# Sparse attention rewritten to work on pairs of heads, with a pair's fifth chunk of transposes in the second PSUM bank, copied by VectorE

## The chip, the cores and the metric

One core of a Trainium2 chip runs the whole program. Its engines are TensorE (PE in the profile, its weight loads PEld), VectorE (DVE), ScalarE (ACT), GpSimd (POOL) and SyncE (SP, which issues the DMAs). The metric is the device time of one execution in microseconds, the median of several; lower is better.

## What is computed

A stack of layers on 512 tokens of width 1024, all in float32. The change lies in the second layer, whose attention has three branches for 16 heads of width 64 in two groups of keys and values, and beside them an attention of 4 heads on 256 memory rows:

```python
def nsa_layer(x, mem, ...):
    h = rms_norm(x, norm_g) @ w_in
    q, kv, gate_logits, z, qm, zm = split_cols(h, NSA_IN_SPLITS)
    ...
    k_cmp = compress_tokens(kc, pe_k, phik_w1, phik_w2)
    v_cmp = compress_tokens(vc, pe_v, phiv_w1, phiv_w2)
    o_cmp, p_cmp = compressed_attention(q, k_cmp, v_cmp, slopes)
    o_slc = selected_attention(q, ks, vs, p_cmp, slopes)
    o_win, _ = banded_attention(q, kw, vw, slopes, WIN_SIZE - 1, 1)
```

Every branch is softmax(q k^T / 8 - slope x distance) v with causal masking. With 512 tokens the selection takes all 8 blocks and the window covers all keys, so "selected" and "window" are both plain causal attention, with keys ks and values vs, and kw and vw. The compressed branch has 31 block keys. The branches are gated and summed, then multiplied by silu(z) and by the output weights.

## The kernel before

Stages follow one another, each closed by a barrier of all engines. Ahead of the attention stand a projection stage, which fills the query tiles q_stack, the keys ks and kw, the values vs and vw, the gates and yT (silu of z), and the stage compress, which makes k_cmp and v_cmp. Behind it stands output_product, the product with the output weights.

**Float32 by parts.** TensorE multiplies in a rounded float32 format in one pass. To keep accuracy a tensor is split into a high part and a low rest. Before, q_stack holds one tile for each head, its high part in partitions 0 to 63 and its low part in 64 to 127 (stack_halves), and a key tile holds its high part twice and its low part twice (twice_halves). A score tile then takes two matmuls over 128 partitions (stacked_scores).

**Units.** nsa_attention makes a list of units and hands it to column_attention with n_sets 1, lag 3, n_buf 4. A unit of kind "table" is one head in one branch: scores of four token tiles of 128, 256, 384 and 512 keys in PSUM banks 0 to 2, scanned by VectorE (add the distance table, take the maximum, one instruction for each tile, L1145), exponentials by ScalarE in place (L1233), reciprocal of the sums times the gate by VectorE (L1184, L1186), scaling by GpSimd (L1299), ten 128x128 transposes by TensorE (L1070) in three chunks in banks 3 to 5, two of which VectorE copies to SBUF (L1201) and one ScalarE (L1253). After two heads the value products of both follow (L1090), on half the columns of the array each. "cmp" is the compressed branch of four heads at once; "plain" is a memory head, scanned at L1150.

What sets the order on TensorE is the loop of passes. In pass k it does:

```python
pe.wait_ge(ready, cnt.pieces[k - n_sets + 1])   # in scores(k): all tiles of unit k - 1 scanned
...
scores(k); turn(k - lag); product(k - lag - 1)
```

VectorE does scan(k), weigh(k - 1), copy(k - lag), finish(k - lag - 1), and where head.at names the pass a split of output weights or of y rows (L228). finish multiplies a finished pair by silu(z) (L1384). GpSimd also builds each head's distance table (L2164). In the first four passes TensorE runs 16 idle_products, matmuls on the identity whose result nobody reads (L168). SyncE issues the zero fill of the expert rows, after unit 20 the first output weights into the free query tiles (load_head), and after the last product the second ones (start_second).

**The head of the next product.** At the end the stage does the first k row of the output product, 12 matmuls (begin_head, L160 to L162). output_product then does rows 1 and 2, runs its rider (transposes of mem_rows, which its own DMA loads first, L2220), and goes on with weights that VectorE rounds and splits (L173, L175).

A later stage, diff_attention, is written in the other style: units of two 64-row score sets, the matmuls of the two in alternation on different halves of the rows (L2341), scans at L2420, in the order DIFF_PAIRS.

## Time and profile before

| | us |
|---|---|
| median of 3 runs | 2972.87 |
| the runs | 2964.62 to 2975.65 |
| the profiled execution | 2974.96 |
| its span, first to last instruction | 2973.0 |
| mean granted TensorE clock | 0.986 of full |

Over the span TensorE is busy 94%, VectorE 64%, ScalarE 41%, GpSimd 12%. The attention stage of the change runs from 763 to 941 us. "Idle before" and the name behind the arrow in a row tell how long the engine waited and which instruction ended the wait.

### The profile page before, as it was taken

To read this page: it belongs to the slowest core of one execution; us is meant where nothing else is said; L and a number is where in the kernel's file an instruction comes from. 1 tells how busy PE (TensorE), PEld (TensorE's weight loads), DVE (VectorE), ACT (ScalarE), POOL (GpSimd) and SP (SyncE) were. 2 spreads that over 40 slices of the span, in tenths; PEclk is the share of its full clock that TensorE was granted. 3 is DMA by queue.
4 is the path that set the end of the run, shared out by engine and by line. 5 is a ranking of instruction groups with operands and counts; after the bars stand their busy time and mean duration, and the time that the engine had idled before them with its cause. 6 is when DMAs were issued, how large, how long until landed. Compare 5 with 4: busy or idle time off the path is not lost. (4 is left out here: it accounts for less than half of the span.)

```text
span 2973.0 us, 35123 instructions
## 1 busy us (share of the span) xinstructions
PE 2789.1 (94%) x13386; PEld 2234.4 (75%) x13386; DVE 1892.3 (64%) x2853; ACT 1213.9 (41%) x2112; POOL 363.9 (12%) x490
## 2 busy tenths in 40 slices
PE   7989999899999899999999899999999999989997
PEld 6768877787666687877887688868787778767885
DVE  5653345463586555766545788864586654668887
ACT  3450132221563214572013577731367201357774
POOL 0120022000452001230000200100123000020002
PEclk9999999999999999999999999999999999999999
DMA  3313212233911232302325899923220223579995
GB/s 123 103 54 94 91 52 75 76 101 90 346 44 64 72 124 75 99 30 85 94 92 201 309 406 409 368 99 128 75 86 31 96 86 99 208 303 370 408 405 189
DMA packets 155549, 465.08 MB, mean 156 GB/s; under 512 B 17366, under 2 KB 34808, under 8 KB 130040
## 3 DMA queue, kind: packets, MB, share of 16 engines
q1 hardware_dynamic: 146600, 430.87, 40.3%
q0 software_dynamic: 8784, 31.99, 2.9%
q8 instruction: 106, 1.74, 0.2%
q14 instruction: 59, 0.48, 0.1%
HBM read 413.01 MB, written 49.81 MB: 156 GB/s over the span
## 5 line engine op out<-in xcount | busy, mean ns | idle before, releaser
L173 DVE CAST weights_r<-weights 128x1024 fp32r<-128x1024 f32 (+4 forms) x248 | 192.2, 775 | 594.3 <-DMA weights<-in_w_in 171.2
L175 DVE TENSOR_TENSOR weights_r<-weights,weights_r 128x1024 fp32r<-128x1024 f32 (+4 forms) x248 | 362.3, 1461 | 8.5
L160 PE MATMUL ps<-x_cols_hi_r,weights_r 128*128 128x512 f32 x832 | 326.2, 392 | 5.0 <-DVE x_cols_lo_r L3428 2.1
L161 PE MATMUL ps<-x_cols_lo_r,weights_r 128*128 128x512 f32 x832 | 324.6, 390 | 0.0
L162 PE MATMUL ps<-x_cols_hi_r,weights_r 128*128 128x512 f32 x832 | 324.4, 390 | 0.0
L160 PEld LDWEIGHTS ps<-x_cols_hi_r,weights_r 128*128 128x128 f32 x832 | 156.6, 188 | 42.7 <-issue 4.2
L162 PEld LDWEIGHTS ps<-x_cols_hi_r,weights_r 128*128 128x128 f32 x832 | 156.5, 188 | 32.7
L161 PEld LDWEIGHTS ps<-x_cols_lo_r,weights_r 128*128 128x128 f32 x832 | 156.7, 188 | 32.0
L1299 POOL TENSOR_SCALAR weights<-weights,weight 128x128 f32<-128x128 f32 (+1 forms) x240 | 120.5, 520 | 390.3 <-DVE weight L1182 315.7
L2678 ACT ACTIVATE sig<-ps 128x512 f32<-128x512 f32 x48 | 28.1, 600 | 331.6 <-PE ps L162 331.6
L160 PE MATMUL ps<-hawk_xT_hi_r,weights_r 128*128 128x512 f32 x368 | 145.3, 395 | 7.7 <-DVE weights_r L175 7.7
L162 PE MATMUL ps<-hawk_xT_hi_r,weights_r 128*128 128x512 f32 x368 | 144.2, 392 | 0.0
L161 PE MATMUL ps<-hawk_xT_lo_r,weights_r 128*128 128x512 f32 x368 | 144.2, 392 | 0.0
L1233 ACT ACTIVATE weights<-weights,minus_top 128x256 f32<-128x256 f32 (+3 forms) x176 | 96.2, 547 | 70.4 <-DVE minus_top L1145 70.4
L160 PE MATMUL ps<-weights_r,block_xT_lo_r 128*128 128x512 f32 x264 | 107.9, 409 | 6.3 <-DVE block_xT_lo_r L3299 6.3
L160 PE MATMUL ps<-expert_hi_r,block_xT_lo_r 128*128 128x512 f32 x264 | 105.5, 400 | 0.0
L160 PE MATMUL ps<-merged_T_r,hidden_T_lo_r 128*128 128x512 f32 x264 | 104.2, 395 | 1.2 <-DVE hidden_T_lo_r L3306 1.2
L162 PE MATMUL ps<-weights_r,block_xT_hi_r 128*128 128x512 f32 x264 | 104.5, 396 | 0.0
L162 PE MATMUL ps<-merged_T_r,hidden_T_hi_r 128*128 128x512 f32 x264 | 103.7, 393 | 0.0
L162 PE MATMUL ps<-expert_hi_r,block_xT_hi_r 128*128 128x512 f32 x264 | 103.1, 391 | 0.0
L160 PE MATMUL ps<-branch_hi_r,weights_r 128*128 128x512 f32 x256 | 100.0, 391 | 3.1 <-issue 3.1
L162 PE MATMUL ps<-branch_hi_r,weights_r 128*128 128x512 f32 x256 | 99.7, 389 | 0.0
(677 smaller groups left out, 6936.9 us busy)
## 6 DMA issues: line engine op xcount, KB each, us to landing
weights<-in_w_in SPq DMA_DIRECT2D x76, 512.0 KB, 4.1
weights<-in_hawk_w_in SPq DMA_DIRECT2D x50, 512.0 KB, 3.9
weights<-in_w_in SPq DMA_DIRECT2D x22, 1024.0 KB, 5.3
x_cols_hi<-in_w_exp_gate SPq DMA_DIRECT2D x22, 1024.0 KB, 7.3
x_cols_lo<-in_w_exp_up SPq DMA_DIRECT2D x18, 1024.0 KB, 8.3
attn_T<-in_w_exp_down SPq DMA_DIRECT2D x18, 1024.0 KB, 8.2
weights<-in_w_exp_down SPq DMA_DIRECT2D x16, 1024.0 KB, 8.6
block_x<-expert_x_rows SPq DMA_DIRECT2D x31, 512.0 KB, 8.8
```

Source lines behind the costliest of these rows:

```text
L160: pe.matmul(out, as_r(left[1]), as_r(right[0]), start=start, stop=False)
L161: pe.matmul(out, as_r(left[0]), as_r(right[1]), start=False, stop=False)
L162: return pe.matmul(out, as_r(left[0]), as_r(right[0]), start=False, stop=stop)
L173: dve.tensor_copy(as_r(hi), lo).then_inc(rounded, 1)
L175: dve.tensor_tensor(as_r(lo), lo, as_r(hi).bitcast(F32), ALU.subtract).then_inc(done, 1)
L1233: act.activation(e(k, p), e(k, p), ACT.Exp, bias=ntop[:, slot, p.stat:p.stat + 1], scale=-1.0, accum_out=total[:, slot, p.stat:p.stat + 1] ...
L1299: ins = pool.tensor_scalar(part(p, e(k, p), i), part(p, e(k, p), i), w[:, p.stat + i:p.stat + i + 1], 1.0, ALU.mult, ALU.mult)
L2678: act.activation(sig[:, j, :], m.ps[:, j * BANK:(j + 1) * BANK], ACT.Sigmoid).then_inc(s.gated, 1)
```

## The change

Names: a step is a pass of the new loop (i in the code), with these units in order: cmp; pair 0 branch 0, pair 0 branch 1, pair 1 branch 0, pair 1 branch 1; mem; cmp; four pair units; mem; cmp; four; cmp; four. That is 22 units in place of 40.

- q_stack holds two heads in one tile, the high part in tile 2n and the low part in tile 2n + 1, written by one instruction each (high_low). Scores become three matmuls over 64 partitions for each head, the two heads in alternation.
- The score tiles of both heads lie in banks 0 to 4 in the order of diff_attention. Each bank is given back after certain scans, not after all.
- The 20 transposes of a unit go in five chunks: bank 5 copied by ScalarE (first, third), bank 6 copied by VectorE (second, fourth, fifth). Products of the unit before stand between the chunks, in two parts. Output lies in bank 7 alone.
- Compressed scores take two matmuls a head (high, low); k_cmp has a copy for each half. Two of the four quads are made before the first unit, two behind it.
- No idle_products. The tail does two k rows of the output product (begun=2), placed between chunks.
- cmp_rows uses the room of kc and vc (one tensor kvc).

```diff
-            nsa_attention(... free=20, at=(25, 27, 29, 31, 33, 35))
+            head_start(... at=(17, 17, 17, 20, 21, 22), begun=2)
...
-                    for k in range(1, ks):
+                    for k in range(head.begun, ks):
...
+    return [bag(bank=5, by="act", turns=turns(0, (0,), 0), copies=[(0, 0, 0, 512)]),
+            bag(bank=6, by="dve", turns=turns(1, (0,), 0), copies=[(1, 0, 0, 512)]),
+            bag(bank=5, by="act", turns=turns(0, (1, 3), 512), copies=[(0, 512, 0, 512)]),
+            bag(bank=6, by="dve", turns=turns(1, (1, 3), 512), copies=[(1, 512, 0, 512)]),
+            bag(bank=6, by="dve", turns=turns(0, (2,), 1024) + turns(1, (2,), 768), copies=[(0, 1024, 0, 256), (1, 1024, 256, 256)])]
...
+            def pair_scores(i):
...
+                for n, pair in enumerate(DIFF_PAIRS):
+                    for bank in sorted({at // BANK for _, _, at in pair}):
+                        if n < 3 and (n != 2 or bank == 4):
+                            bank_free(bank)
+                    if n == 3:
+                        pe.wait_ge(s.scored, marks[i] + 4)
+                    for step in range(3):
+                        for c, t, at in pair:
+                            half, toks, cols = slice(64 * c, 64 * c + 64), slice(t * P, (t + 1) * P), slice(0, (t + 1) * P)
+                            part, low = ((1, 0), (0, 1), (0, 0))[step]
+                            mm = pe.matmul(ps[:, at:at + (t + 1) * P], as_r(qs[half, 2 * u.pair + part, toks]), as_r(k[half, g, low, cols]),
+                                           start=step == 0, stop=step == 2)
...
+            for i in range(1, n_units + 3):
+                if i < n_units:
+                    scores(i)
+                if i == n_units:
+                    pe.wait_ge(s.scanned, marks[n_units])
+                    head_row(0)
+                if 2 <= i < n_units + 2:
+                    turn(i - 2, (0, 1))
+                if i >= 3:
+                    product(i - 3, 0)
+                if 2 <= i < n_units + 2:
+                    turn(i - 2, (2, 3))
+                if i >= 3:
+                    product(i - 3, 1)
+                if 2 <= i < n_units + 2:
+                    turn(i - 2, (4,))
+                if i == n_units + 1:
+                    head_row(1)
...
+            for i in range(n_units + 4):
+                if 3 <= i < n_units:
+                    dve.wait_ge(s.turned, all_chunks[i - 2])
+                if i < n_units:
+                    scan(i, (0, 1))
+                if i >= 4:
+                    finish(i - 4)
+                if 1 <= i <= n_units:
+                    weigh(i - 1)
+                if 2 <= i < n_units + 2:
+                    copy(i - 2, 0)
+                if i < n_units:
+                    scan(i, (2, 3, 4, 5))
+                if 2 <= i < n_units + 2:
+                    copy(i - 2, 1)
+                if i < n_units:
+                    scan(i, (6, 7))
+                if 2 <= i < n_units + 2:
+                    copy(i - 2, 2)
+                split_head(dve, s, head, [n for n, at in enumerate(head.at) if at == i])
```

ScalarE runs exponent(i) in the same thirds (0, 1), (2 to 5), (6, 7) with its copies between; GpSimd scales unit i, head by head, as soon as it is weighed.

TensorE in the middle of the stage, before. Two heads of the window branch (kw): eight score matmuls of one head, ten transposes of another, again for the next head, then the value products.

```order
L1052 MATMUL ps<-kw_r,q_stack_r 128x128 x2
L1052 MATMUL ps<-kw_r,q_stack_r 128x384 x2
L1052 MATMUL ps<-kw_r,q_stack_r 128x256 x2
L1052 MATMUL ps<-kw_r,q_stack_r 128x512 x2
L1070 MATMUL ps<-ident,weights 128x128 x10
L1052 MATMUL ps<-kw_r,q_stack_r 128x128 x2
```

The same place now, from the first value products of the window branch on.

```order
L2314 MATMUL ps<-ident,weights 128x128 x8
L2343 MATMUL ps<-by_key,vw 64x512 x2
L2343 MATMUL ps<-by_key,vw 64x384 x2
L2314 MATMUL ps<-ident,weights 128x128 x8
L2343 MATMUL ps<-by_key,vw 64x128 x2
L2343 MATMUL ps<-by_key,vw 64x256 x2
```

The products no longer stand in one piece: eight transposes and a half of the products alternate, and all 24 score matmuls of the next pair (L2273) stand together ahead of them.

VectorE in the middle of the stage, before: the end of one head's scans, its weighing (L1184, L1186), two copies, and the first scan of the next head. ISA is the scan and the read of its maximum.

```order
L1145 ISA weights,minus_top<-ps,table_rows 128x512
L1145 ISA minus_top 128x1
L1184 RECIPROCAL weight<-total 128x4
L1186 TENSOR_TENSOR weight<-weight,gates 128x4
L1201 COPY weights<-ps 128x512 x2
L1145 ISA weights,minus_top<-ps,table_rows 128x128
```

VectorE now: the second copy of a unit (the fourth chunk), the last two of eight scans, the fifth chunk's copies, and the next unit's first scan.

```order
L2437 COPY by_key<-ps 128x512
L2396 ISA weights,minus_top<-ps,table_rows 128x384
L2396 ISA minus_top 128x1
L2396 ISA weights,minus_top<-ps,table_rows 128x128
L2396 ISA minus_top 128x1
L2437 COPY by_key<-ps 128x256 x2
L2396 ISA weights,minus_top<-ps,table_rows 128x512
```

The copies stood together behind a head's scans and now stand between the scans of a pair.

TensorE at the end of the stage, before: the last value products, then the head row.

```order
L1090 MATMUL ps<-more_scores,vw 64x256 x2
L1090 MATMUL ps<-more_scores,vw 64x128 x2
L160 MATMUL ps<-q_stack_r,nsa_yT_r 128x512
L161 MATMUL ps<-q_stack_r 128x512
L162 MATMUL ps<-q_stack_r 128x512
```

TensorE at the end now: the last fifth chunk, the second head row (its last three matmuls), the last value products.

```order
L2314 MATMUL ps<-ident,weights 128x128 x4
...
L160 MATMUL ps<-q_stack_r,nsa_yT_r 128x512
L161 MATMUL ps<-q_stack_r 128x512
L162 MATMUL ps<-q_stack_r 128x512
L2343 MATMUL ps<-by_key,vw 64x512 x2
L2343 MATMUL ps<-by_key,vw 64x384 x2
L2343 MATMUL ps<-by_key,vw 64x128 x2
L2343 MATMUL ps<-by_key,vw 64x256 x2
```

The head rows moved ahead of the last products, and the stage ends on products that VectorE still has to take.

## Rows read from the trace of the kernel before

**Rows 1.** Windows: us, busy time and count per engine, PEclk, DMA share, GB/s.
```profile
767.00:937.00 170.00, 153.69 (x992) 108.17 (x990) 135.38 (x443) 102.13 (x336) 89.78 (x171) 0.98 0.36 141
797.76:840.82 43.06, 39.56 (x261) 27.59 (x262) 34.79 (x114) 26.61 (x91) 24.80 (x50) 1.00 0.61 243
```

**Rows 2.** Waits, 767 to 937: waiting engine, releaser, total us, times, longest.
```profile
PEld ps L1052 <- DVE minus_top L1145: 11.7, 19, 2.0
PEld ps L1070 <- POOL weights L1299: 8.5, 20, 1.3
```

**Rows 3.** Timeline, VectorE, gated outputs: start us, us, engine, line, operation.
```profile
797.76 0.69 DVE L1384 TENSOR_TENSOR nsa_yT<-ps,nsa_yT 128x512 f32<-128x512 f32 x1 [0.61 <-PE ps L1090]
...
840.82 0.69 DVE L1384 TENSOR_TENSOR nsa_yT<-ps,nsa_yT 128x512 f32<-128x512 f32 x1 [0.61 <-PE ps L1090]
...
937.29 0.69 DVE L1384 TENSOR_TENSOR nsa_yT<-ps,nsa_yT 128x512 f32<-128x512 f32 x1 [2.48 <-PE ps L1090]
```

**Rows 4.** Differential attention: timeline; in the middle matmuls of 1297 to 1301.
```profile
1298.13 0.19 PEld L2341 LDWEIGHTS ps<-k_hi_r,merged_T_r 64*128 64x128 f32 x2 [0.17 <-issue]
...
L2341 PE MATMUL ps<-k_hi_r,attn_T_r x8: 270/306/394, 1298.7 to 1300.1; 64*128 64x512 f32 x2, 64*128 64x256 f32 x2, 64*128 64x384 f32 x2, 64*128 64x128 f32 x2
...
1294.02 0.69 DVE L2420 CUSTOM_DVE_ANT_0 weights<-ps,mask 128x512 f32<-128x512 f32 x1 [0.24 <-DVE weights L2433]
...
1297.68 1.93 DVE L2433 SCALAR_TENSOR_TENSOR weights<-weights,weight 128x512 f32<-128x512 f32 x4
...
1299.85 0.69 DVE L2420 CUSTOM_DVE_ANT_0 weights<-ps,mask 128x512 f32<-128x512 f32 x1 [0.24 <-PE ps L2341]
```

**Rows 5.** Timeline, TensorE's weight loads: scores, transposes, compressed product, value products.
```profile
820.99 1.11 PEld L1052 LDWEIGHTS ps<-kw_r,q_stack_r 128*128 128x128 f32 x8 [0.81 <-issue]
...
928.42 1.07 PEld L1070 LDWEIGHTS ps<-ident,weights 128*128 128x128 f32 x10 [1.29 <-POOL weights L1299]
...
929.46 0.30 PEld L1090 LDWEIGHTS ps<-cmp_by_key,v_cmp 128*128 128x128 f32 x2
...
930.52 0.20 PEld L1090 LDWEIGHTS ps<-weights,vs 128*64 128x64 f32 x4 [0.76 <-issue]
...
932.83 1.07 PEld L1070 LDWEIGHTS ps<-ident,weights 128*128 128x128 f32 x10 [0.17 <-issue]
```

**Rows 6.** Timeline, VectorE: first scan, weighing's end and copies, split of a row.
```profile
822.00 0.29 DVE L1145 CUSTOM_DVE_ANT_0 weights<-ps,table_rows 128x128 f32<-128x128 f32 x1 [0.21 <-PE ps L1052]
...
823.94 1.28 DVE L1201 COPY weights<-ps 128x512 f32<-128x512 f32 x2
...
881.10 1.17 DVE L228 TENSOR_TENSOR nsa_yT_r<-nsa_yT,q_stack_r 128x512 fp32r<-128x512 f32 x1 [0.31 <-ACT q_stack_r L220]
```

**Rows 7.** Timeline, ScalarE and GpSimd, one head: exponentials, copy, scaling.
```profile
822.34 0.40 ACT L1233 ACTIVATE weights<-weights,minus_top 128x128 f32<-128x128 f32 x1 [1.60 <-DVE minus_top L1145]
...
824.63 0.36 ACT L1253 ACTIVATE weights<-ps 128x256 f32<-128x256 f32 x1
...
824.12 2.06 POOL L1299 TENSOR_SCALAR weights<-weights,weight 128x128 f32<-128x128 f32 x4 [1.93 <-DVE weight L1186]
```

**Rows 8.** Timeline, TensorE at the start: compressed scores, then the first head's scores.
```profile
763.16 3.64 PE L1096 MATMUL ps<-q_stack_r,k_cmp 128*32 128x512 f32 x32 [1.05 <-PEq L91]
...
769.62 1.10 PEld L1052 LDWEIGHTS ps<-ks_r,q_stack_r 128*128 128x128 f32 x8 [0.70 <-DVE weights L1139]
```

**Rows 9.** Timeline, TensorE in the next stage: row 1, mem_rows, second weights.
```profile
941.05 0.47 PE L160 MATMUL ps<-q_stack_r,nsa_yT_r 128*128 128x512 f32 x1 [0.87 <-PEq L91]
...
946.80 0.86 PEld L2220 LDWEIGHTS ps<-ident,mem_rows 128*128 128x128 f32 x8 [0.45 <-DMA mem_rows<-in_mem]
...
947.63 0.19 PEld L160 LDWEIGHTS ps<-weights_r,nsa_yT_r 128*128 128x128 f32 x1
```

**Rows 10.** Windows, with the columns of the first group.
```profile
886.00:890.00 4.00, 2.69 (x15) 2.36 (x13) 3.89 (x8) 1.43 (x3) 1.92 (x5) 0.79 0.02 4
```

More of the change, by code:

```diff
@@ L189, with head_start @@
 HEAD_SIGNALS = ("head_loaded*2", "head_rounded", "head_split")
-def head_start(m, w, col, hi, lo, ks, product, second, y=(), free=None, at=(), spans=None):
+def head_start(m, w, col, hi, lo, ks, product, second, y=(), free=None, at=(), spans=None, begun=1):
     spans = spans or [(0, col, 512)]
@@ L1999, in _ @@
                                bias=off[:, n:n + 1]).then_inc(s.hidden, 1)
[L2000 removed]
+            act.wait_ge(s.offset, 10)
             for g in range(NSA_GROUPS):
@@ L2021, in low, with high_low, hi @@
         return ins
+    return bag(hi=hi, low=low)
+def high_low(dst, per, scale):
+    def hi(act, bank, c, j):
+        return act.activation(as_r(dst[:, 2 * (per * c + j), :]), bank, ACT.Copy, scale=scale)
+    def low(dve, bank, c, j):
+        n = 2 * (per * c + j)
+        return dve.scalar_tensor_tensor(out=as_r(dst[:, n + 1, :]), in0=bank, scalar=scale, in1=as_r(dst[:, n, :]).bitcast(F32),
+                                        op0=ALU.mult, op1=ALU.subtract)
     return bag(hi=hi, low=low)
@@ L2123, in alibi_slopes @@
     return [float(v) for v in np.exp2(-8.0 * np.arange(1, n + 1) / n).astype(np.float32)]
-def nsa_attention(nc, m, a, qs, ks, kw, k_cmp, vs, vw, v_cmp, gates, yT, moe, tables, memory, head):
-    causal, cmp_tab, zeros = tables
-    with Tensors(nc) as sb:
+PAIR_SCANS = ((0, 3, 0, 2), (1, 3, 1536, 2), (0, 2, 512, 6), (0, 0, 896, 6), (1, 1, 1280, 8), (0, 1, 1024, 8), (1, 2, 2048, 8), (1, 0, 2432, 8))
+PAIR_FREE = {0: 1, 3: 2, 1: 4, 2: 6, 4: 8}
+MEM_SCANS = ((0, 0, 0), (1, 0, 1536), (0, 2, 512), (1, 2, 2048))
@@ new lines, in mem_chunks, with nsa_units @@
+def mem_chunks():
+    return [bag(bank=5 + c, by="dve" if c else "act", turns=[(c, t * N_MEM + j * P, t * P) for t in range(TT)], copies=[(c, j * 512, 0, 512)])
+            for j in range(MT) for c in range(2)]
+def nsa_units():
+    units = []
+    for q in range(NSA_HEADS // 4):
+        if q in (1, 2):
+            units.append(bag(kind="mem", quad=q, pair=q - 1, branch=1, marks=4, sides=2, chunks=mem_chunks(), free={b: ("exped", n) for b, n in MEM_FREE.items()}))
+        units.append(bag(kind="cmp", quad=q, pair=0, branch=0, marks=1, sides=1, free={0: ("scanned", 1)}, chunks=[
+            bag(bank=5, by="act", turns=[(0, t * P, t * P) for t in range(TT)], copies=[(None, 0, 0, 512)])]))
+        for pair in (2 * q, 2 * q + 1):
+            for branch in range(2):
+                units.append(bag(kind="pair", quad=q, pair=pair, branch=branch, marks=8, sides=2, chunks=pair_chunks(),
+                                 free={b: ("scanned", n) for b, n in PAIR_FREE.items()}))
+    return units
@@ new lines, in nsa_attention @@
+def nsa_attention(nc, m, a, qs, ks, kw, k_cmp, vs, vw, v_cmp, gates, yT, moe, tables, memory, head, cmp_rows):
+    causal, cmp_tab, zeros = tables
+    qms, kms, vm = memory
+    ps, units, width = m.ps, nsa_units(), 1280
+    n_units = len(units)
+    room = [flat(w[:, :, :]) for w in m.w_slots]
+    marks, sides, all_chunks = (running(f(u) for u in units) for f in (lambda u: u.marks, lambda u: u.sides, lambda u: len(u.chunks)))
+    by_act, by_dve = (running(sum(c.by == by for c in u.chunks) for u in units) for by in ("act", "dve"))
+    made = running(u.kind != "cmp" for u in units)
+    outs = running(u.kind != "cmp" and u.branch == 1 for u in units)
+    unit_at = {(u.kind, u.quad if u.kind == "cmp" else u.pair, u.branch): i for i, u in enumerate(units)}
+    slopes = alibi_slopes(NSA_HEADS)
+    with Tensors(nc) as sb, stage(nc, "cmp_made", "cmp_copied", "scored", "scanned", "exped", "weighed", "scaled", "turned", "copied_act", "copied_dve",
+                                  "multiplied", "out_taken", "step", "tabled", "quad_tabled", "cleared", *HEAD_SIGNALS) as (block, s):
@@ L2173, in nsa_attention @@
-        column_attention(nc, m, units, 1, 3, 4, 4, "alone", tables, zero_rows=(moe.x_rows, moe.y_rows), zeros=zeros, idle=(6, 4, 4, 2), head=head, n_keys=4,
-                         cmp_scores=[[(k_cmp[:, q // 2, :], as_r(qs[:, 4 * q + i, :]).bitcast(F32)) for i in range(4)] for q in range(NSA_HEADS // 4)])
+        cmp_keys = sb("cmp_by_key", [P, 2, SEQ])
+        places_ = [room[n // 3][:, n % 3 * width:(n % 3 + 1) * width] for n in range(6)]
+        e_places = (places_[0:2], places_[4:6], places_[2:4])
@@ new lines, in nsa_attention, with e, e_piece, e_mem @@
+        keys = [[sb("by_key", [P, width])[:, :] for _ in range(2)] for _ in range(2)]
+        ntop, total, wt = (sb(n, [P, 2, 16]) for n in ("minus_top", "total", "weight"))
+        def e(i, c):
+            return e_places[i % 3][c]
+        def e_piece(i, c, t):
+            return e(i, c)[:, CAUSAL_COL[t]:CAUSAL_COL[t] + (t + 1) * P]
+        def e_mem(i, c, t, n=1):
+            return e(i, c)[:, t * N_MEM:(t + n) * N_MEM]
+        def stat(tensor, i, c, t, n=1):
+            return tensor[:, i % 2, c * TT + t:c * TT + t + n]
@@ new lines, in blocks, with chunk_copies, finished @@
+        def blocks(i):
+            return e(i, 0)[:, 0:SEQ].rearrange("p (a n) -> p a n", n=32)
+        def chunk_copies(i, chunk):
+            u = units[i]
+            for c, to, at, n in chunk.copies:
+                dst = cmp_keys[:, u.quad % 2, :] if c is None else keys[i % 2][c][:, to:to + n]
+                yield dst, ps[:, chunk.bank * BANK + at:chunk.bank * BANK + at + n]
+        def finished(i):
+            return units[i].kind != "cmp" and units[i].branch == 1
+        @block.sync
@@ new lines, in _ @@
+        def _(sp):
+            for dram in (moe.x_rows, moe.y_rows):
+                sp.dma_start(dram.rearrange("(b p) d -> p b d", p=P),
+                             zeros[:, :].unsqueeze(1).broadcast_to([P, MAX_BLOCKS, D])).then_inc(s.cleared, 16)
+            sp.wait_ge(s.scored, marks[unit_at["pair", 3, 1] + 1])
+            load_head(sp, s, head)
+            sp.wait_ge(s.turned, all_chunks[n_units - 2])
+            start_second(sp, m, head)
+            sp.wait_ge(s.cleared, 32)
+        @block.tensor
```

304 lines of the change are left out of this document (257 added, 47 removed).

## The prediction

> **What bounds the kernel now.** I first asked which engine is full in the stretch that the change rewrites. The windows show it [rows 1]: in the 170 us of the sparse attention stage TensorE is busy 153.69, VectorE 135.38, ScalarE 102.13, GpSimd 89.78. Busy matmuls include modelled ends, so I looked next at what TensorE waits for [rows 2]: 11.7 us on the weight loads of the scores for the last scan of the head before, 8.5 us on the transposes for GpSimd's scaling. So the stage is a TensorE chain with holes. There is one score set (n_sets 1), so a head's scores wait until VectorE has scanned the whole head before. Third, its pace [rows 3]: the first pair's gated output is taken at 797.76, the third pair's at 840.82, the last at 937.29. One round (a memory pair, a compressed unit, two head pairs with two branches each) takes 43.06 us.
>
> **Prices.** A unit of the new kernel is two heads of one branch. TensorE: 24 score matmuls on 64 rows, two at a time. The later differential attention of this same kernel issues just that [rows 4]: first at 1298.13, last at 1300.1, so 2.0 us. Before, two heads need two rounds of eight of 1.11 us [rows 5] and the gap to the transposes, 2.3 us. Ten transposes take 1.04 us (928.42 to 929.46), the compressed product 1.06 us less start-up (I take 0.85, an estimate from a 512-column fp32 product of 0.43 us per pass), the eight value products 2.31 us (930.52 to 932.83) [rows 5]. None of these changes in number. A unit of the first branch (A) thus costs 2.0 + 2.15 + 3.15 = 7.3 us, one of the second (B) 2.0 + 2.15 + 2.3 = 6.45. Memory pair: 1.9, 1.75, 1.75; compressed: 0.45, 0.45, 0.
>
> VectorE: eight scans and the weights of two heads take 3.66 us from 1294.02 to 1297.68 [rows 4]; of four scans and one weighing 1.94 (822.00 to 823.94), so one weighing of two is saved, some 0.2 us [rows 6]. Two 512-column copies are 1.28 [rows 6]; the fifth chunk is two of 256, 0.7 by estimate (half each and a start), and ScalarE would pay about as much, its 256-column copy being 0.36 [rows 7]. With the gated output every second unit (0.3) a pair unit costs VectorE 3.66 + 1.2 + 0.7 + 0.3 = 5.9. ScalarE: four exponentials 2.29 (822.34 to 824.63) [rows 7], so 4.6 and two copies below 0.6: 5.7. GpSimd: 2 x 2.06 [rows 7] and on A two tables: 5.4. TensorE's average of 6.9 is the largest, so giving the fifth chunk to VectorE is hidden by TensorE; if that cover went, it would cost 0.7 us a unit.
>
> **The start.** Compressed scores are now two matmuls a head instead of one; 16 took 3.64 us [rows 8]. The second half of them runs while VectorE scans the compressed unit, but their ScalarE copies end about 771.4, so the first pair's scores start at about 771.5 instead of 769.62 [rows 8]. Then I walked steps 1 to 3. Step 1: scans need 3.3 us and the compressed weighing 1.1, to 776.8. Step 2: its weighing waits for ScalarE's eight exponentials, to 781.7. Step 3: GpSimd's second side is ready only at 783.9, so the first copy of VectorE is late; fourth-step scores start at 787.7.
>
> **The sum from there**, each step at its fullest engine, written as scores + transposes of two units back + products of three back. Step 4: 7.3. Steps 5 to 10 (memory, compressed, A, B, A, B): 1.9 + 2.15 + 2.3 = 6.35; 0.45 + 2.15 + 3.15 = 5.75; 2.0 + 1.75 + 2.3 = 6.05; step 8 has only 4.2 on TensorE and is set by ScalarE and the scan chain, 4.9; step 9 by VectorE (3.7 + 1.9 + 0.6), 6.2; step 10, 7.3. Together 36.55. Steps 11 to 16 are the same, 36.55. Step 17 carries three splits of the output projection's rows at 1.17 us [rows 6]: VectorE 2.15 + 0.4 + 1.9 + 3.4 = 7.85; 18: 7.3; 19: 5.0; 20, VectorE with one split: 7.3; 21: 7.3; together 34.75. Tail: a head row of the projection is 12 matmuls, 2.75 us (24 from 941.05 to 946.6) [rows 9]; 22: 2.75 + 2.15 + 2.3 = 7.2; 23: 2.15 + 3.15 + 2.75 = 8.05; 24: 2.3; together 17.55. All: 7.3 + 36.55 + 36.55 + 34.75 + 17.55 = 132.7. Hand-overs between engines: the differential attention repeats in 5.83 us (1294.02 to 1299.85) for 3.66 + 1.93 = 5.59 of VectorE [rows 4], 0.24 a step; I take 0.2 x 20 = 4.0. End of products: 787.7 + 136.7 = 924.4.
>
> **The clock.** The granted clock falls to 0.79 of full over 886 to 890, after TensorE waited there [rows 10]; that is part of the time at 1.2 instead of 2.4 GHz. The new steps 1 to 3 leave TensorE 8.4 us of work in 16, with no matmuls to fill the idle time (the change drops them), so I expect the low level there: 3 us, and 1.5 us after steps 17 and 20. The Trainium skill's page "TensorE: Matmul & The Clock Gate" (Part 1) says the throttled rate is the default and activity releases it; by that rule alone all of steps 1 to 4 would be at half rate, some 7 us in place of 3, and the row agrees as to direction. Bounds: 0 and 10. Products then end at 928.9; the last gated output 0.8 and the change of stage 1.0 put the next stage at 930.7, against 941.05 [rows 9]: 10.3 us gained.
>
> **Behind the stage.** begun=2 takes the second head row, 2.75 us, out of the next stage. That returns nothing: its weights' products start at 947.63, right behind transposes that start at 946.80, when the DMA of mem_rows has landed [rows 9]. With 2.75 us less ahead of it TensorE waits instead, and may lose clock: 1.0 us lost, bounds -1 and +3. In the projection before the stage the q tiles are rounded by one ScalarE and one VectorE instruction instead of two each; TensorE does not wait for them, 0. An extra small copy in compress: 0.1. SyncE's queue holds the same DMAs in the same order: the zero fill of the expert rows first, then the head's weights, issued after the fourth pair's scores and needed only by step 20, then the second weights, issued in step 21 instead of after the last product. Nothing waits behind them, 0; the last of these may speed the DMA of mem_rows, which is the -1 above.
>
> Net: 10.3 - 1.0 = 9.3 us. The profiled execution took 2974.96 us (span 2973.0), 2.1 above the median of the runs shown, 2972.87. So 2965.7 for an execution like it and **2964 us** for the median. Half a per cent, 15 us, is about what a measurement of this kernel can tell from no change.
>
> **Rivals.**
> (1) The forecast, 2957 to 2971: 0.52.
> (2) Steps overlap over their borders and the clock stays up. Two scores ahead of the transposes give slack; for it speaks that TensorE's own work from 787.7 is only 120.9 us, 11.9 below my sum. Against it: scores wait for scans and scans for scores in each step. All of it and the 4.5 of clock would give 2964 - 16 = 2948; half, 2956. Chance 0.20.
> (3) The fifth chunk's wait decides. It now shares the second bank with the fourth, so TensorE waits for VectorE's copy of the fourth, which stands behind four scans (1.4 us), and the next scores queue behind it. The point is whether the fourth chunk is turned before those scans are through. By my walk it is turned 0.2 us or more after them, so that the wait is 0.2. If earlier, up to 1.4 us x 16 units = 22 us: 2986. Chance 0.08. The Trainium skill's page "Trainium Kernel Development and Optimization" (Best Practices) says that tiling speeds up compute but not PSUM evacuation. In that stricter reading VectorE paces every unit; this case's differential attention, where VectorE is full, agrees, and here it would mean 5.9 a unit, below TensorE's 6.9, so the rule bites only with such waits.
> (4) Every light step (3, 9, 15, 17, 20) costs a stretch at 1.2 GHz of 2 us: +10, 2974. For it: [rows 10]. Against: 797.76 to 840.82 had holes too and lost no clock [rows 1]. Chance 0.15.
> (5) The 64-row matmuls of the two heads do not run beside each other: 16 x 2.0 us more, 2996. The rows of the differential attention speak against it [rows 4]: 0.02.
> (6) The new steps hold but the start loses more (GpSimd, ScalarE), and it ends level, 2972: 0.03.
>
> **How the numbers follow.** Faster by over 0.5% is below 2958: most of (2) and a little of (1), 0.25. Slower by over 0.5% is above 2988: (5) and the far end of (3), 0.05. The rest is 0.70. The range reaches from the middle of (2) to beyond (4), 2950 to 2978, and leaves out 0.1 on either side.
>
> **What would show it.** In the profile after: first pair scores at 771.5; first value products near 790 (right if within 2 us); a round of 37 to 38 us between gated outputs in place of 43.06; TensorE's wait before each fifth chunk near 0.2 us; granted clock below 1 in 775 to 792; the next stage at about 931; its first weights' products 6.6 us after its start as before. The forecast is wrong if the round is below 35 or above 40 us, if TensorE waits over 0.5 us for the fourth chunk's copy, or if clock losses are spread over all light steps.

## The result: slower, where little change was forecast

| | us, median | lowest to highest |
|---|---|---|
| before | 2972.87 | 2964.62 to 2975.65 |
| after | 2995.06 | 2990.53 to 3000.02 |

Each is the median of five runs. The ratio is 1.0082, with an interval of 1.0063 to 1.0102: slower by 22 us, beyond the half per cent that the prediction named. A second measurement (experiment 11) gave 1.0077, 1.0064 to 1.0090. The forecast was 2964 us, the range 2950 to 2978. The profiled execution after has a span of 2995.8 us, 22.8 above that of before.

The first question is where. The timeline of the changed kernel gives the start of the sparse attention's first pair scores (PE L2273), the gated outputs on VectorE (L2445, which was L1384 in [rows 3]) and the first instructions of the next stage:

```profile
770.71 2.21 PE L2273 MATMUL ps<-ks_r,q_stack_r 64*128 64x512 f32 x24 [0.72 <-ACT kvc L2506]
...
827.67 0.69 DVE L2445 TENSOR_TENSOR nsa_yT<-ps,nsa_yT 128x512 f32<-128x512 f32 x1
...
875.28 0.69 DVE L2445 TENSOR_TENSOR nsa_yT<-ps,nsa_yT 128x512 f32<-128x512 f32 x1
...
959.80 0.69 DVE L2445 TENSOR_TENSOR nsa_yT<-ps,nsa_yT 128x512 f32<-128x512 f32 x1 [4.30 <-PE ps L2343]
...
961.35 0.47 PE L160 MATMUL ps<-q_stack_r,nsa_yT_r 128*128 128x512 f32 x1 [1.60 <-PEq L91]
...
968.15 0.78 PE L160 MATMUL ps<-weights_r,nsa_yT_r 128*128 128x512 f32 x1
```

A time of day can't be compared between two profiles as it stands: what comes ahead of the stage takes a little less or more from one execution to the next. So I count from an instruction at the start of the stage that both kernels have, VectorE's first add of the compressed unit. First before, then after:

```profile
767.43 0.69 DVE L1137 TENSOR_TENSOR weights<-ps,table_quads 128x512 f32<-128x512 f32 x1 [5.99 <-PE ps L1046]
...
766.46 0.69 DVE L2408 TENSOR_TENSOR weights<-ps,table_quads 128x512 f32<-128x512 f32 x1 [5.99 <-PE ps L2293]
```

From there the first pair scores come after 4.25 us, where the forecast had walked 4.07 (771.5) and the first head's came after 2.19 [rows 8]. The next stage starts at 961.35, where it was 941.05 [rows 9], that is after 194.9 us in place of 173.6: the attention stage is 21.3 us longer. What follows it is 2.5 us longer, what comes ahead of it 1.0 shorter; that makes the 22.8. A round (827.67 to 875.28) takes 47.6 us; it took 43.06 [rows 3], and 37 to 38 were forecast. The windows answer to [rows 1]; their columns are the same (us, then busy time and count of TensorE, its weight loads, VectorE, ScalarE, GpSimd, then the granted clock, DMA share, GB/s):

```profile
827.67:875.28 47.61, 40.30 (x294) 27.19 (x293) 31.53 (x107) 28.50 (x93) 24.74 (x49) 0.93 0.05 18
767.00:961.00 194.00, 161.62 (x1136) 106.69 (x1128) 120.70 (x406) 110.06 (x341) 89.31 (x174) 0.91 0.32 125
836.00:844.00 8.00, 5.83 (x33) 4.87 (x34) 5.73 (x22) 5.08 (x17) 4.10 (x8) 0.57 0.01 2
812.00:816.00 4.00, 4.00 (x10) 0.85 (x9) 0.33 (x1) 0.22 (x1) 3.54 (x8) 0.61 1.02 413
```

VectorE has less to do than before (120.7 us in place of 135.4), and no engine is full. The granted clock is 0.91 over the stage, where it was 0.98: some stretches run at 1.2 GHz. So the next question is who waits. Waits of 770 to 960 (engine, line, releaser, total us, times, longest):

```profile
PE ps L2314 <- ACT by_key L2501: 15.2, 5, 3.7
DVE weights L2396 <- POOL table_rows L2532: 11.0, 3, 3.7
PEld ps L2273 <- DVE minus_top L2396: 6.2, 9, 1.9
PE ps L2339 <- DVE nsa_yT L2445: 6.0, 4, 2.0
```

The scores' wait for the scans of the unit before, on which the forecast had built (11.7 us in [rows 2]), is down to 6.2, as wanted. Three others, of which the forecast had nothing, are about as large or larger: TensorE for ScalarE's copy, VectorE for the distance tables, and the compressed product for the output. The timeline of step 9, a light step (the unit three back is the compressed one, so TensorE has no value products to do), shows the first two of them, which are one chain across four engines:

```profile
828.77 4.11 POOL L2551 TENSOR_SCALAR weights<-weights,weight 128x512 f32<-128x512 f32 x8 [3.94 <-DVE weight L2428]
832.96 1.32 POOL L2532 TENSOR_SCALAR table_rows<-causal 128x512 f32<-128x512 f32 x2
...
834.41 0.69 DVE L2396 CUSTOM_DVE_ANT_0 weights<-ps,table_rows 128x512 f32<-128x512 f32 x1 [3.68 <-POOL table_rows L2532]
...
836.57 0.57 ACT L2501 ACTIVATE by_key<-ps 128x512 f32<-128x512 f32 x1
...
837.29 1.94 PE L2314 MATMUL ps<-ident,weights 128*128 128x128 f32 x8 [3.69 <-ACT by_key L2501]
840.11 1.09 PE L2314 MATMUL ps<-ident,weights 128*128 128x128 f32 x4 [0.87 <-DVE by_key L2437]
841.12 3.29 PE L2273 MATMUL ps<-kw_r,q_stack_r 64*128 64x512 f32 x24
```

Read from the top: GpSimd scales the first branch of a pair (4.11 us) and only then makes the next pair's two distance tables. VectorE's first scan needs them and waits 3.68 us. The first two exponentials queue behind the scan, and ScalarE's copy of the first chunk behind the exponentials. TensorE wants the bank of that copy for its third chunk and stands 3.69 us. Then it runs at the lower clock: eight transposes in 1.94 us, where 1.09 is usual, 24 score matmuls in 3.29 in place of 2.21. TensorE's wait is put down to ScalarE's copy, but its cause is an instruction on GpSimd, three hand-overs back. VectorE's wait of 3.7 us for the tables ends at 834, 882 and 923, and a like one at 784, in step 3: the profile puts that one down to TensorE, but GpSimd's tables are ready at 783.90 and the scan starts at 784.03.

The third wait is that of the compressed product (L2339) for the output bank. The timeline of step 6:

```profile
808.94 0.68 DVE L2408 TENSOR_TENSOR weights<-ps,table_quads 128x512 f32<-128x512 f32 x1
809.66 0.69 DVE L2409 TENSOR_REDUCE minus_top<-weights 128x16 f32<-128x512 f32 x1
810.38 0.69 DVE L2410 TENSOR_TENSOR weights<-weights,minus_top 128x512 f32<-128x512 f32 x1
810.99 0.68 DVE L2445 TENSOR_TENSOR nsa_yT<-ps,nsa_yT 128x512 f32<-128x512 f32 x1
...
811.81 1.10 PE L2339 MATMUL ps<-cmp_by_key,v_cmp 128*128 128x512 f32 x2 [2.01 <-DVE nsa_yT L2445]
812.84 3.26 PE L2343 MATMUL ps<-by_key,vs 128*64 128x512 f32 x8
```

The change has one bank for the output where the kernel before used two in turn. VectorE does the compressed unit's three instructions first and takes the finished pair's output behind them, so the next pair's products wait 2.01 us. Eight of them then take 3.26 us in place of 1.72, at a clock of 0.61. That second loss does not come every time: the same wait, 2.02 us before 861.03, is followed by products at full clock (1.72 us).

### The profile page after: what moved, and what is told of

The parts are those of the page before. It is cut to its first block and busy times, and to the rows that moved or that the text cites. A ratio compares the mean times of both kernels' runs of the same rounds, so it can differ in the third digit from the quotient of the medians.

```text
span 2995.8 us, 35393 instructions
## 1 busy us (share of the span) xinstructions
PE 2796.0 (93%) x13514; PEld 2232.4 (75%) x13514; DVE 1871.5 (62%) x2808; ACT 1217.8 (41%) x2108; POOL 362.2 (12%) x490
## 3 DMA queue, kind: packets, MB, share of 16 engines
q1 hardware_dynamic: 146600, 430.87, 40.1%
## 5 line engine op out<-in xcount | busy, mean ns | idle before, releaser
L173 DVE CAST weights_r<-weights 128x1024 fp32r<-128x1024 f32 (+4 forms) x248 | 191.6, 772 | 594.6 <-DMA weights<-in_w_in 171.7
L3225 POOL DMA_INDIRECT expert_x_rows<-x,slot x16 | 26.4, 1653 | 587.4 <-DVE n_late L3313 583.1
L2476 ACT ACTIVATE weights<-weights,minus_top 128x512 f32<-128x512 f32 (+3 forms) x128 | 70.5, 552 | 44.4 <-DVE minus_top L2396 44.4
```

The source lines that it names most:

```text
L173: dve.tensor_copy(as_r(hi), lo).then_inc(rounded, 1)
L2476: act.activation(e_piece(i, c, t), e_piece(i, c, t), ACT.Exp, bias=stat(ntop, i, c, t), scale=-1.0, accum_out=stat(total, i, c, t)).then_i ...
L3225: pool.indirect_dma_start(out=moe.x_rows, out_offset=bass.IndirectOffsetOnAxis(ap=moe.slot[:, i * TT + t:i * TT + t + 1], axis=0), in_=x[: ...
```

## Experiments: the two queues apart and together

Theory T: the late tables cost most of the loss. Theory O: the late output costs a part of its own. Rival B: the shared bank of the fifth chunk, the named change, is what costs.

**1, tables early.**

```diff
             for i, u in enumerate(units):
+                if u.kind == "pair" and u.branch == 0 and u.pair + 1 < NSA_HEADS // 2:
+                    build(2 * u.pair + 2)
+                    build(2 * u.pair + 3)
                 pool.wait_ge(s.weighed, i + 1)
...
-                if u.kind == "pair" and u.branch == 0 and u.pair + 1 < NSA_HEADS // 2:
-                    build(2 * u.pair + 2)
-                    build(2 * u.pair + 3)
```

> Edit: GpSimd makes the two distance tables of the next head pair before it waits for the weights of the first branch (it idles there), not after scaling that branch. Same work, same results. Theory T (tables): in the changed kernel VectorE's first scan waits for a table at the start (784.03) and three times later (3.7 us each), the copies of the first chunk queue behind it, TensorE stands 3.7 us and then runs its next 5 us of matmuls at the 1.2 GHz level. It expects the waits for table_rows gone and 11 to 24 us less than the changed kernel, so +11 to -2 us against the kernel before (ratio 0.9995 to 1.0035). Rival B (the fifth chunk's bank) and rival O (the single output bank) expect that the stall only moves: within 4 us of the changed kernel, ratio 1.006 to 1.009.

Measured: 2980.96 us, against 2972.59 of the kernel before on the same chip; ratio 1.0024, 1.0013 to 1.0034. Both measurements of the changed kernel lie 5 to 6 thousandths higher, some 16 us, in the middle of what T expected and far from B. From the first compressed add to the next stage's first rounding on ScalarE the stage takes 179.9 us; it is 194.9 in the changed kernel. The round is 44.1 us (825.96 to 870.06), and TensorE's wait in step 9 shrinks from 3.69 to 0.82. So the chain is real, and at its head stand two instructions of 1.32 us together, in the wrong place of a queue.

```profile
832.71 1.06 PE L2314 MATMUL ps<-ident,weights 128*128 128x128 f32 x8 [0.82 <-ACT by_key L2501]
...
835.34 2.21 PE L2273 MATMUL ps<-kw_r,q_stack_r 64*128 64x512 f32 x24
```

**2, output first.**

```diff
+                if i >= 4:
+                    finish(i - 4)
                 if i < n_units:
                     scan(i, (0, 1))
-                if i >= 4:
-                    finish(i - 4)
```

> Edit: VectorE takes a finished pair's gated output before the first two scans of a step, not behind them (behind all three instructions of a compressed unit). Theory O (output bank): TensorE's products of the next pair wait for this one bank, 2.0 us at 811.8 and 861.0, 1.4 at 909.4, 0.6 at 949.4, 0.4 for memory pairs, and the clock falls behind the long ones (0.61 in 812 to 816). It expects 6 to 10 us less than the changed kernel: ratio to the kernel before 1.004 to 1.0055. Theory T alone expects under 2 us, since the time comes back at the next table wait: 1.007 to 1.0085.

Measured: 2989.98 us, ratio 1.0062, 1.0044 to 1.0080, some 6 us below the changed kernel: between what O and what T alone expected, with an interval that reaches into both. The rows decide it: the stage takes 187.0 us, where the changed kernel takes 194.9, VectorE takes the output at 809.25, and the compressed product starts without a wait:

```profile
810.08 1.10 PE L2339 MATMUL ps<-cmp_by_key,v_cmp 128*128 128x512 f32 x2
```

**3, both edits.**

> Edit: both of the above, the early tables and the output ahead of the scans. If T and O are two separate losses their gains add: 17 to 34 us less than the changed kernel, ratio to the kernel before 0.996 to 1.002, and rounds of 38 to 42 us between gated outputs in place of 47.6. If one hides the other, this run is no faster than the better of the two alone.

Measured: 2970.14 us, ratio 0.9993, 0.9983 to 1.0002: the whole loss is gone. The next stage starts at 938.18, the stage takes 171.7 us, and the round is 40.5 us (819.53 to 860.05). By the length of the stage the tables alone give 15.0 us, the output alone 7.9, both 23.2: they add, and neither hid the other.

**4 and 8, the fifth chunk back on ScalarE and the first bank**, in the changed kernel and in the kernel with both edits.

```diff
-            bag(bank=6, by="dve", turns=turns(0, (2,), 1024) + turns(1, (2,), 768), copies=...)]
+            bag(bank=5, by="act", turns=turns(0, (2,), 1024) + turns(1, (2,), 768), copies=...)]
```

> Edit: the fifth chunk of transposes goes to the first bank and is copied by ScalarE, all else as in the changed kernel. Rival B expects that this frees VectorE of 0.76 us a unit and TensorE of its waits for the copy of the fourth chunk (4.0 us in 5 waits): 4 to 16 us less, ratio to the kernel before 1.003 to 1.007. Theories T and O expect the table and output waits to stay as they are, and a change of at most 3 us either way: 1.007 to 1.0095.

> Edit, on the kernel with both edits: the fifth chunk to the first bank and ScalarE. With the table and output waits gone the choice of the bank could show at last. For it: TensorE waits 4.4 us for VectorE's copies in that kernel. Against it: nearly all of those are at the light steps, where ScalarE is the later engine. Expected within 4 us either way of the kernel with both edits, ratio 0.998 to 1.001; 4 us or more less would say that the second bank is the wrong choice once the waits are gone, 4 or more above it that it is the right one.

Measured: 2997.32 us (1.0082, 1.0065 to 1.0099) on the changed kernel, nothing that can be told from it; 2978.92 us (1.0021, 1.0011 to 1.0031) on both edits, by the ratios some 8 us slower than these alone, where 4 had been set as the mark. So B falls, and the sign is the other way: the second bank and VectorE are the right choice, but one can see it only once the two queues no longer cover it. The rows of experiment 8 say why; the wait before the fifth chunk is 1.78 us in place of 0.88, and it now exists in full steps too. Over 770 to 950 TensorE waits 15.8 us for copies, where it was 10.7 (6.3 for ScalarE's, 4.4 for VectorE's):

```profile
831.10 1.06 PE L2314 MATMUL ps<-ident,weights 128*128 128x128 f32 x8 [1.09 <-ACT by_key L2501]
833.95 0.63 PE L2314 MATMUL ps<-ident,weights 128*128 128x128 f32 x4 [1.78 <-ACT by_key L2501]
...
849.37 0.63 PE L2314 MATMUL ps<-ident,weights 128*128 128x128 f32 x4 [0.45 <-ACT by_key L2501]
```

**9, the value products in one piece**, on both edits. The forecast had priced them as one piece.

```diff
                 if i >= 3:
                     product(i - 3, 0)
+                    product(i - 3, 1)
                 if 2 <= i < n_units + 2:
-                    turn(i - 2, (2, 3))
-                if i >= 3:
-                    product(i - 3, 1)
-                if 2 <= i < n_units + 2:
-                    turn(i - 2, (4,))
+                    turn(i - 2, (2, 3, 4))
```

> Edit, on the kernel with both edits: a unit's value products in one piece behind the first two chunks, then the third, fourth and fifth chunk's transposes; before, the second half of the products stood between the fourth chunk and the fifth. The prediction priced the products as one piece of 2.31 us; in the trace the two pieces take 2.6. If the cover is what counts (the second half hides VectorE's copy of the fourth chunk, which shares its bank with the fifth), TensorE now waits 0.9 us or more before each fifth chunk: 8 to 18 us more than with both edits, ratio 1.002 to 1.0055. If the split is what costs, 3 to 5 us less: 0.9975 to 0.9985.

Measured: 2979.56 us, ratio 1.0017, 1.0008 to 1.0026: some 7 us slower than both edits, by the ratios, just under the lower end of what the cover theory said. Both effects are there. This is a step of the kernel with both edits, with no wait after its first row, then the same step of experiment 9:

```profile
829.79 0.63 PE L2314 MATMUL ps<-ident,weights 128*128 128x128 f32 x4 [0.88 <-DVE by_key L2437]
830.35 2.21 PE L2273 MATMUL ps<-kw_r,q_stack_r 64*128 64x512 f32 x24
832.49 1.09 PE L2314 MATMUL ps<-ident,weights 128*128 128x128 f32 x8
833.42 1.02 PE L2339 MATMUL ps<-cmp_by_key,v_cmp 128*128 128x512 f32 x2
834.37 1.72 PE L2343 MATMUL ps<-by_key,vs 128*64 128x512 f32 x8
836.03 1.09 PE L2314 MATMUL ps<-ident,weights 128*128 128x128 f32 x8
837.05 0.87 PE L2343 MATMUL ps<-by_key,vs 128*64 128x128 f32 x8
838.00 0.63 PE L2314 MATMUL ps<-ident,weights 128*128 128x128 f32 x4
838.38 0.36 PE L2285 MATMUL ps<-mem_T_lo_r,mem_T_hi_r 128*128 128x256 f32 x1
```

```profile
837.83 2.37 PE L2343 MATMUL ps<-by_key,vs 128*64 128x512 f32 x16
840.14 1.09 PE L2314 MATMUL ps<-ident,weights 128*128 128x128 f32 x8
842.11 0.63 PE L2314 MATMUL ps<-ident,weights 128*128 128x128 f32 x4 [0.87 <-DVE by_key L2434]
```

In one piece the products take 2.31 us from start to start (837.83 to 840.14). In two they take 1.66 + 0.95 = 2.61: 0.15 us for each of the two changes of tile shape that the split adds (128x64 to the transposes' 128x128 and back). The same cost stands between transposes and scores: four transposes ahead of the 64-row scores take 0.56 (829.79 to 830.35), four ahead of the memory pair's 128-row scores 0.38 (838.00 to 838.38). The Trainium skill's page "TensorEngine Tiling (Array Packing)" (Tiling Modes, Key Properties) says that changing the tiling mode drains TensorE; by that rule these steps should cost more than their parts, and the trace agrees, at 0.15 to 0.18 us a change. Yet the split is worth its price: without it TensorE waits 14.6 us in 17 waits for VectorE's copies, 0.87 us in nearly every pair unit, where it was 4.4 us in 6.

**5, the second row back in the next stage**, on both edits.

```diff
-                              ..., at=(17, 17, 17, 20, 21, 22), begun=2)
+                              ..., at=(17, 17, 17, 20, 21, 22))
...
-                if i == n_units + 1:
-                    head_row(1)
```

> Edit, on the kernel with the early tables and the output first: the output projection's second row goes back to the next stage, as in the kernel before. The prediction's term says that having it early returns nothing, since that stage waits for the DMA of mem_rows either way. In the kernel with both edits TensorE waits 3.2 us there and its first nine matmuls of the weights take 0.63 us at the lower clock. If the term is right the attention stage ends 2.75 us earlier, the weights' products start 6.6 us after the stage's start in place of 7.1, at the full clock: 3 to 5 us less than with both edits, ratio to the kernel before 0.9975 to 0.9985. If the early row does return its time, the two cancel: 0.999 to 1.0.

Measured: 2968.85 us, ratio 0.9989, 0.9978 to 1.0000. That is 1 us below both edits, less than expected, and the intervals overlap; the time alone doesn't tell. The rows at the border do, first of the kernel with both edits, then of experiment 5:

```profile
938.18 0.47 PE L160 MATMUL ps<-q_stack_r,nsa_yT_r 128*128 128x512 f32 x1 [1.60 <-PEq L91]
...
944.43 1.09 PE L2600 MATMUL ps<-ident,mem_rows 128*128 128x128 f32 x8 [3.24 <-DMA mem_rows<-in_mem]
945.28 0.48 PE L160 MATMUL ps<-weights_r,nsa_yT_r 128*128 128x512 f32 x1
```

```profile
935.00 0.47 PE L160 MATMUL ps<-q_stack_r,nsa_yT_r 128*128 128x512 f32 x1 [1.59 <-PEq L91]
...
941.24 1.09 PE L2598 MATMUL ps<-ident,mem_rows 128*128 128x128 f32 x8 [0.52 <-DMA mem_rows<-in_mem]
942.08 0.47 PE L160 MATMUL ps<-weights_r,nsa_yT_r 128*128 128x512 f32 x1
```

Either way the weights' products start 7.1 us after the stage's start, behind the DMA of mem_rows. Done early, the row only turns work into a wait, 3.24 us in place of 0.52. The other profiles scatter: the distance is 5.7 to 7.1 us in the ten with the early row (6.80 in the changed kernel) and 6.3 to 7.1 in the three without, 6.4 and 6.7 on average. So the prediction's term, that the row's 2.75 us return nothing there, holds to some tenths. The stage of experiment 5 is 5.9 us shorter (165.8 for 171.7), of which 2.6 lie at the start and have another cause (experiment 6). So that the early row costs its 2.75 us in the stage is read from the rows; the median does not show it.

**6, a fill in step 3**, on both edits: ten matmuls on the identity into the free output bank behind the first two chunks, seven behind the third and fourth.

```diff
+                if i == 3:
+                    idle_products(pe, m, 10)
...
+                if i == 3:
+                    idle_products(pe, m, 7)
```

> Edit, on the kernel with both edits: 17 transposes of the identity into the free output bank in step 3, where TensorE waits for the copies of the compressed unit (10 behind its first chunk's transposes, 7 behind the third and fourth). Theory of the clock: the low level in 784 to 792 follows on the gaps there and costs 2.5 us (scores 3.89 us in place of 2.21, transposes 1.52 in place of 1.09); with the fill it stays up and the kernel is 2 to 3 us faster than with both edits, ratio 0.998 to 0.999. If the low clock has another cause, the scores stay at 3.9 us and the fill costs up to 1 us.

Measured: 2973.10 us, ratio 0.9999, 0.9990 to 1.0009: no gain. In its windows the clock is 1.00 from 775 to 799, and the scores of step 4 take 2.19 us in place of 3.89. But that is no proof of the fill: experiment 5, whose instructions up to there are those of the kernel with both edits, has no low clock in step 4 either. Windows of both edits, then of experiment 5:

```profile
780.00:784.00 4.00, 2.74 (x26) 2.03 (x25) 2.71 (x12) 4.00 (x16) 3.27 (x8) 1.00 1.02 397
784.00:788.00 4.00, 2.39 (x12) 1.86 (x12) 2.69 (x13) 3.55 (x13) 3.92 (x8) 0.65 1.02 413
788.00:792.00 4.00, 4.00 (x27) 3.33 (x25) 2.36 (x8) 1.85 (x7) 0.92 (x3) 0.50 1.02 412
```

```profile
780.00:784.00 4.00, 4.00 (x26) 3.06 (x25) 3.65 (x19) 4.00 (x16) 3.79 (x8) 0.57 1.02 406
784.00:788.00 4.00, 2.30 (x22) 1.73 (x20) 2.75 (x13) 4.00 (x14) 3.24 (x8) 1.00 1.01 398
788.00:792.00 4.00, 3.12 (x33) 2.58 (x31) 3.02 (x12) 2.99 (x12) 3.29 (x7) 1.00 1.02 412
```

The low stretch lies in 784 to 792 in the one, ahead of steps in which TensorE is full, and in 780 to 784 in the other, ahead of waits that can absorb it; and the stage of the other starts 2.7 us later (first compressed add at 769.21, not 766.48), so that the shift is larger still. The first gated output comes 39.3 us after that add in the one and 36.7 in the other. So between two executions of the same instructions the place of a low stretch can move by several microseconds, and that moved the start by 2.6 us. It does not always: in the two profiles of the changed kernel the clock of the three windows from 784 on is 0.69, 0.50, 0.53 and 0.67, 0.50, 0.55. What the fill itself does stays open.

**7, ScalarE's first copy ahead of the exponentials**, on both edits.

```diff
+                if i >= 2:
+                    copy(i - 2, 0)
                 if i < n_units:
                     exponent(i, (0, 1))
-                if i >= 2:
-                    copy(i - 2, 0)
```

> Edit, on the kernel with both edits: ScalarE copies the first chunk of two units back before the first two exponentials of the step, not behind them. What is left of TensorE's waits there (6.3 us in 7 waits for that copy, up to 1.5, and 4.4 us for VectorE's copies) is put down to that order. If so 3 to 6 us less than with both edits, ratio 0.997 to 0.9985. If the exponentials are the chain, TensorE's waits move to the transposes that need the scaled weights, and it is within 2 us either way or slower.

Measured: 2970.30 us, ratio 0.9993, 0.9984 to 1.0003, the same as without it. The wait for that copy in step 9 falls from 1.10 to 0.60, that for VectorE's fourth chunk rises from 0.88 to 1.35, and the round goes from 40.5 to 40.1. That is the rival's outcome: the wait moves on. Its profile showed the stage 4.3 us shorter, 3.1 of it at the start, where the clock happened to stay up; the expectation of the next run took that as a gain, which was wrong.

**10 and 11, all five together, and the changed kernel again.**

> Edit: early tables, output first, second row back in the next stage, fill in step 3, ScalarE's first copy ahead of the exponentials: all five together, the candidate. By the stage's own rows the last three gave 3.2, 1.6 and 3.3 us; if they add to the 2.5 us that the kernel with both edits is below the kernel before, 8 to 11 us less than the kernel before: ratio 0.9963 to 0.9975. If they hide one another, 0.998 to 0.9995.

> The changed kernel once more, on the chip of the others, so that their distance from it is taken on one chip: 1.0075 to 1.009 times the kernel before if the first measurement holds.

Measured on one chip: before 2973.97 us; all five edits 2965.53, ratio 0.9970, 0.9958 to 0.9982; the changed kernel 2997.93, ratio 1.0077, 1.0064 to 1.0090. Both lie inside what was expected: of the two ranges for the five edits, the one in which the gains add. The version with five edits is faster than both kernels, by 8 and 32 us. Most of it comes from the first two edits; the other three were not each shown to pay. The changed kernel's second profile repeats the waits of the first (15.2, 11.1 and 6.0 us for the three named above).

## Why the prediction was wrong, point by point

**What bounds the stage.** That TensorE has the most work was right and is still so (152.5 us busy of 169 in the stage with both edits). The step that failed is "each step at its fullest engine": it adds up durations and takes for granted that an instruction is ready when its engine is free. The prediction gave GpSimd 5.4 us on a unit of the first branch, below TensorE's 7.3, and dropped it. As a sum that is right: GpSimd is busy 24.7 of 47.6 us in the round. But its two tables stand last in that 5.4, and the next pair's first scan stands right behind them. In a light step (3 at the start, 9, 15, 20) the scan comes due before 4.11 + 1.32 us are over. The code has both facts: the tables behind the scaling, the wait ahead of the scan. Step 9, 6.2 us in the forecast, took 10.75. The forecast's own time for the stage, from the first compressed add (767.43 to 930.7), is 163.3 us; it took 194.9. Of these 31.6 us, 23.2 go with the two edits of experiment 3.

**The output.** The prediction charged VectorE 0.3 us a unit for it and no wait to TensorE. With a single bank and three instructions ahead of it, it cost 6.0 us in waits and, by the stage's length in experiments 1 to 3, 7.9 us alone and 8.2 on top of the tables (23.2 - 15.0).

**The prices of TensorE.** With both edits the stage takes 171.7 us, still 8.4 more than the forecast's 163.3, though step 4 starts only 1.4 us later than walked (21.7 us after the first add, 20.3 forecast). Its scores then run at the low clock, so that the first value products start at 793.9, not near 790. Steps 5 to 10 take 40.51 us in place of 36.55: 7.04, 7.39, 6.64, 4.59, 6.82 and 8.03 us, where 6.35, 5.75, 6.05, 4.9, 6.2 and 7.3 were forecast. 2.4 us of the 40.51 are waits for copies, in steps 6 and 9. Step 10 has no wait at all and takes 8.03, where 7.3 was forecast: 2.14 for the scores (2.0), 2.61 for the value products (2.31), and the rest on transposes cut into three groups and on the compressed product (0.95 for 0.85). The prices were taken from rows where each kind ran in one piece, and the changes of shape between the new, smaller pieces had none. That is a mis-sized term, 0.7 us in this step and 0.6 to 0.7 in steps 5 and 7. (The 2.31 us, which the prediction has for eight value products, are for sixteen in its own rows; the price is right as used.) So the version with both edits, 2970 us, lies inside the forecast's range, but not for its reason: its round of 40.5 us is beyond the 40 that the prediction itself named as a sign of being wrong.

**The clock.** 3 us at the start and 1.5 behind steps 17 and 20 together were allowed. After the change it is low in 784 to 796, 836 to 844, 884 to 892 and 924 to 932, behind each of the four table waits, and in 812 to 816, behind the first output wait but not behind the others. In steps 9, 15 and 20 it costs 2.4 us each (in step 9, 0.85 and 0.46 for the transposes and 1.08 for the scores), at the start 3.6, behind the output 1.6: some 12 us, where 4.5 were allowed. So the prediction's own sign of failure, clock losses spread over the light steps, came true, and rival (4) was right on where (but for step 17) and not on why: most of it goes with the waits. With both edits 2.6 us remain at the start, the first round is at 1.00, and the second at 0.96, with 0.82 and 0.76 in 868 to 876 behind copy waits (1.09 and 0.88 us) that cost no clock in the first. Why the clock fell behind some of these short waits and not behind others stays open.

**The rivals.** (3), the shared bank: not the cause. The wait is 0.9 us, over the 0.5 that the prediction had named as a sign of being wrong (0.2 was forecast), but it comes only in light steps and once, with 0.5, in the tail, 4.0 us in all. Its cover, the second half of the products, is real (experiment 9). (5), 64-row matmuls not side by side: wrong, 2.14 us. (2), overlap over the steps' borders: nothing shows it. The case that came, an instruction queued behind work that it does not need, was under no rival but by name in (6), at 0.03. The chance of slower, 0.05, was far too small for a rewrite that sets a new order on five engines.

**Right were** the start up to the first pair scores (4.25 us for 4.07), that the second head row returns next to nothing in the next stage, that TensorE hides the fifth chunk in full steps, and that nothing ahead of the stage costs time: the first compressed add comes at 766.5 to 770.5 in the profiles of all versions of the changed kernel, at 767.4 before.

## What to carry to other kernels

For every wait that a rewrite puts into the code, ask what stands ahead of the instruction that releases it, in that engine's own queue, and walk the lightest step, not the average one: the queue's sum may be half of the step and the released work still late. Put work that someone else waits for (a table, the emptying of the only output bank) ahead of work that only has to be done in the step. When a price is taken from a long run of like matmuls and the new code cuts the run up, add a price for each change of tile shape (0.15 to 0.18 us here), and then check what the cut covers before undoing it. Between two profiles compare lengths from a common instruction, not times of day: taken as times of day, the two edits' gains seem to be 13.6 and 6.6 us, in place of 15.0 and 7.9, and the pair seems to give 3 us more than its parts.

## What the runs showed of the hardware

A change of tile shape on TensorE costs 0.15 to 0.18 us in this stage (2.61 against 2.31 for sixteen value products with two changes more, 0.56 against 0.38 for four transposes).

Behind waits of 3.2 to 3.7 us the granted clock fell each of the four times, to 0.50 to 0.69 over 8 to 12 us (0.57 over 836 to 844), which is mostly the 1.2 GHz level. Behind a wait of 2.0 us it fell at 812 (0.61, and 0.59 in the second profile) and stayed at 1.00 at 861, in both profiles of the changed kernel; with the tables early it fell behind both such waits (0.75 in 808 to 812, 0.78 in 856 to 860).

Where a low stretch falls can differ between executions of the same instructions: 784 to 792 in one, 780 to 784 in another, with 2.6 us between their first gated outputs. A difference of that size between two single profiles of the start is no proof of an edit's effect.
